# First layer of a two-model kernel: POOL's elementwise parts moved to DVE, squares ahead of weight splits, decays regrouped

## What is computed

```python
hn = rms_norm(h, norm_mix_g[0])
xx = token_shift(x) - x                       # x is hn
xr, xw, xk, xv, xa, xg = [x + xx * mix[i] for i in range(6)]
r, k, v = xr @ w_r, xk @ w_k, xv @ w_v
w_log = -softplus(-(w0 + tanh(xw @ w1) @ w2)) - 0.5
a = sigmoid(a0 + (xa @ a1) @ a2)
g = sigmoid(xg @ g1) @ g2
kk = heads(k * k_k); kk = kk / maximum(norm(kk), 1e-12)
k = k * (1 + (a - 1) * k_a)
decay = exp(-exp(w_log))                      # then the scan with r, decay, k, v, -kk, kk * a
```

## Time and profile before

| | |
|---|---|
| median of 3 runs | 3311.23 us (3302.97 to 3314.74) |
| the profiled execution | 3308.2 us, its span 3306.0 us |
| PE busy | 3093.4 us (94%) |
| DVE busy | 1885.4 us (57%) |
| ACT busy | 1278.8 us (39%) |
| POOL busy | 698.1 us (21%) |
| mean granted clock of PE | 0.964 |
| chain that ended last | PE 75%, DVE 13%, ACT 4%, DMA 3%, issue 2%, POOL 1% |

### The profile page before, as it was taken

How to read it: one execution, slowest core, us unless ns; L and a number is a source line. 1 busy time by engine, 2 the same in 40 slices (tenths; PEclk the granted TensorE clock), 3 DMA queues, 4 the chain that set the end, 5 groups by cost and what they waited for, 6 DMA issues and landing times.

```text
span 3306.0 us, 46816 instructions
## 1 busy us (share of the span) xinstructions
PE 3093.4 (94%) x19356; PEld 2711.4 (82%) x19356; DVE 1885.4 (57%) x2692; ACT 1278.8 (39%) x2186; POOL 698.1 (21%) x682
## 2 busy tenths in 40 slices
PE   5989999999999988889999989898999999999998
PEld 5987878789999978789999987655788887878887
DVE  6676545546666562653666665786553544355353
ACT  3555555433223342553432335432332333243231
POOL 3233222122112240111320231311120211112020
PEclk9889999999999989889999999999999999999999
DMA  2210000024554421002446452100222232222222
GB/s 89 77 53 34 1 1 1 34 84 141 175 182 138 166 68 61 1 1 71 148 149 211 136 183 89 51 1 7 83 88 97 90 102 83 96 83 88 97 90 89
DMA packets 79652, 284.40 MB, mean 86 GB/s; under 512 B 8496, under 2 KB 9392, under 8 KB 78672
## 3 DMA queue, kind: packets, MB, share of 16 engines
q1 hardware_dynamic: 79440, 281.41, 25.4%
HBM read 275.02 MB, written 6.36 MB: 85 GB/s over the span
## 4 chain that ended last, share of the span: by engine, by line
PE 75%; DVE 13%; ACT 4%; DMA 3%; issue 2%; POOL 1%; SPq 0%; DVEq 0%; ACTq 0%; POOLq 0%
PE psum L347 54%; DMA araw<-d_ada 3%; DVE wlo L304 2%; PE psum L1216 2%; PE psum L382 2%; PE psum L1237 1%; DVE xt L692 1%; PE psum L1248 1%; DVE araw L428 1%; DVE rdn L2650 1%; PE psum L1245 1%; PE psum L1920 1%; PE psum L2574 1%; DVE mxw L2629 1%; ACT whi L297 1%
## 5 line engine op out<-in xcount | busy, mean ns | idle before, releaser
L304 DVE TENSOR_TENSOR wlo<-wraw,whi 128x1024 fp32r<-128x1024 f32 (+2 forms) x398 | 526.2, 1349 | 652.5 <-ACT whi L297 644.1
L297 ACT CAST whi<-wraw 128x1024 fp32r<-128x1024 f32 (+2 forms) x398 | 395.7, 1022 | 529.4 <-PE psum L347 482.3
L428 DVE CUSTOM_DVE_ANT_0 araw<-araw,cond 128x1024 f32<-128x1024 f32 x112 | 137.4, 1237 | 82.3 <-DMA araw<-d_ada 82.2
L347 PE MATMUL psum<-f1xh,whi 128*128 128x264 f32 x704 | 144.5, 287 | 7.4 <-DVE f1xl L542 3.9
L347 PE MATMUL psum<-f0xh,whi 128*128 128x264 f32 x704 | 143.9, 286 | 7.9 <-DVE wlo L304 4.1
L347 PE MATMUL psum<-f1xh,wlo 128*128 128x264 f32 x704 | 143.9, 286 | 0.0
L347 PE MATMUL psum<-f3xh,whi 128*128 128x512 f32 x352 | 139.8, 397 | 4.2 <-DVE f3xl L538 4.2
L347 PE MATMUL psum<-f2xh,whi 128*128 128x512 f32 x352 | 139.7, 397 | 4.2 <-DVE f2xl L538 4.2
L347 PE MATMUL psum<-f1xl,whi 128*128 128x264 f32 x704 | 143.5, 285 | 0.0
L347 PE MATMUL psum<-f0xh,wlo 128*128 128x264 f32 x704 | 143.4, 285 | 0.0
L347 PE MATMUL psum<-f0xl,whi 128*128 128x264 f32 x704 | 143.0, 285 | 0.0
(11 more groups left out here) (518 smaller groups left out, 8937.7 us busy)
## 6 DMA issues: line engine op xcount, KB each, us to landing
wraw<-d_w SPq DMA_DIRECT2D x357, 512.0 KB, 3.4
araw<-d_ada SPq DMA_DIRECT2D x112, 512.0 KB, 3.3
wraw<-d_w SPq DMA_DIRECT2D x32, 384.0 KB, 3.1
hn<-d_h SPq DMA_DIRECT2D x4, 528.0 KB, 7.3
hres<-d_h SPq DMA_DIRECT2D x1, 2112.0 KB, 8.4
spill<-hres SPq DMA_DIRECT2D x1, 2112.0 KB, 7.4
hres<-spill SPq DMA_DIRECT2D x1, 2112.0 KB, 8.4
cond<-d_cond SPq DMA_DIRECT2D x2, 1024.0 KB, 4.9
```

Source lines behind the costliest of these rows:

```text
L297: e.copy(whi[0:rows, n % NH, 0:kt * cols], wraw[0:rows, n % NR, 0:kt * cols]).then_inc(*w_hi.up(n))
L304: e.tensor_tensor(wlo[0:rows, n % NH, 0:kt * cols], wraw[0:rows, n % NR, 0:kt * cols], whi[0:rows, n % NH, 0:kt * cols].bitcast(F32), ALU. ...
L347: ins = e.matmul(psum[0:bw, b0 + nb * len(sl) + si, 0:ln], l_ if z == 2 else h_, (xp.lo if z == 1 else xp.hi)[:, k, o:o + ln], start=k == ...
L428: e.tensor_tensor_reduce(out=w, in0=w, in1=self.c[:, col, :], scale=1.0, scalar=0.0, op0=ALU.mult, op1=ALU.add, accum_out=ada[:, ly, blk, ...
```

## The change

It does five things, all in the first layer's projections.

- The low parts of the odd blocks (48 blocks in all, 24 of them on POOL before), the even blocks of `xx`, the decays' subtraction, and the operands `b` and `r` all go from POOL to DVE. POOL keeps one memset here.
- The low part of a block comes one block later than its mix (`rest_dve`), and the weight split between the halves of a mix stands ahead of the half's last low part (`mix_split_dve`).
- At the start ACT squares first, then splits chunks 0 and 1, then takes the root, then splits chunk 2. DVE adds first, then splits chunks 0 and 1; chunk 2 comes after the last mix of k.
- On ACT the decays' exponentials stand two at a time behind each pair of `wr` (0 to 5); 6, 7 and `Fc` go into the operand loop, `square(1)` behind the sigmoids. On DVE decays 6 and 7 go behind mix 3.
- One split on each engine goes behind the small matrix g1's outputs.

```diff
         def mix_dve(e, i, ks):
             for k in ks:
...
-                for q in ([k - 1] if k % 2 else []):
-                    e.wait_ge(*m_hi.at(i, q))
-                    e.tensor_tensor(x.lo[:, q, :], xt_of(i, q), x.hi[:, q, :].bitcast(F32),
-                                    ALU.subtract).then_inc(*m_lov.up(i, q))
+                if k > ks[0]:
+                    rest_dve(e, i, k - 1)
+
+        def rest_dve(e, i, k):
+            x = mixed(i)
+            e.wait_ge(*m_hi.at(i, k))
+            e.tensor_tensor(x.lo[:, k, :], xt_of(i, k), x.hi[:, k, :].bitcast(F32), ALU.subtract).then_inc(*m_lo.up(i, k))
+
+        def mix_split_dve(e, i, ks, n):
+            mix_dve(e, i, ks)
+            w_split_dve(e, n)
+            rest_dve(e, i, ks[-1])
...
-        def mix_pool(e, i, ks=range(1, 8, 2)):
...
             rms_square(e, "r0", lambda k: hn[:, k, 1:L + 1], sq0, lambda e, k: e.wait_ge(d_h4[k // 2], 16), range(8))
+            w_split_act(e, 0)
+            w_split_act(e, 1)
             rms_root(e, "r0", L, rt0, 0)
+            w_split_act(e, 2)
...
                 keep(e, "wr", j, 4 * (j % 2), rT, r_out)
-                if j:
-                    decay(2 * j - 2)
-                    decay(2 * j - 1)
+                if j < 3:
+                    decay(2 * j)
+                    decay(2 * j + 1)
             w_split_act(e, chunk("wv", 0, 1))
...
-            e.wait_ge(*p_sc.at(7, 4))
             square(0)
-            square(1)
-            decay(6)
-            decay(7)
-            e.activation(Fc[:, :, :], fa[:, :, :], ACT.Exp, scale=-KAPPA).then_inc(*p_fc.up(0))
             scale(0)
             scale(1)
...
-            mix_dve(e, 4, range(4))
-            w_split_dve(e, n + NH)
-            mix_dve(e, 4, range(4, 8))
-            w_split_dve(e, n + NH + 1)
+            mix_split_dve(e, 4, lo, n + NH)
+            mix_split_dve(e, 4, hi, n + NH + 1)
...
+                e.tensor_tensor(RA[:, 0, k, :], lc, RA[:, 0, k, :], ALU.subtract).then_inc(*p_sc.up(k, 5))
-            for j in range(4):
+            for j in range(3):
                 w_split_dve(e, chunk("wr", j, 0) + NH - 1)
                 decay(2 * j)
...
+            w_split_dve(e, chunk("wr", 3, 0) + NH - 1)
+            mix_split_dve(e, 3, lo, chunk("wr", 3, 1) + NH - 1)
+            mix_split_dve(e, 3, hi, chunk("wv", 0, 1))
+            decay(6)
+            decay(7)
...
+                e.tensor_tensor(a_, nr, a_, ALU.mult).then_inc(*up("b"))
                 e.wait_ge(*p_ls.at(m))
                 e.tensor_tensor(k_, k_, ls, ALU.mult).then_inc(*up("K"))
-                e.wait_ge(*p_b.at(m))
+                e.wait_ge(*p_op.at("b", m))
                 e.scalar_tensor_tensor(out=a_, in0=a_, scalar=v("kk", m), in1=ls, op0=ALU.mult, op1=ALU.mult).then_inc(*up("B"))
+                e.wait_ge(*p_e.at(m))
+                e.tensor_tensor(rT(m), rT(m), LC_[:, m, :], ALU.mult).then_inc(*up("r"))
```

More of the change, by code:

```diff
@@ L633, in program @@
         d_cr = sem("d_cr")
-        h_n = sig("h_n", [x for k in range(8) for x in ([("n", k)] + ([("x", k)] if k % 2 else []))])
-        xx_p = sig("xx_p", [(k,) for k in range(0, 8, 2)])
+        h_n = sig("h_n", [("n", 0)] + [x for k in range(8) for x in ([("n", k + 1)] if k < 7 else []) + [("x", k)]])
         MT = [(i, k) for i in MIX for k in range(8)]
@@ L638, in program @@
         m_hi = sig("m_hi", MT)
-        m_lov = sig("m_lov", [x for x in MT if x[1] % 2 == 0])
-        m_lop = sig("m_lop", [x for x in MT if x[1] % 2])
+        m_lo = sig("m_lo", MT)
         k_out = sig("kept", [(nb,) for nb in range(8)])
@@ L651, in program @@
         p_s = sig("p_s", [(k,) for k in range(8)])
-        p_sc = sig("p_sc", [(k, i) for k in range(8) for i in range(5)])
-        p_L3 = sig("p_L3", [(k,) for k in range(8)])
+        p_sc = sig("p_sc", [(k, i) for k in range(8) for i in range(6)])
         p_l3 = sig("p_l3", [(k,) for k in range(8)])
@@ L663, in program @@
         p_mka = sig("p_mka", [(0,), (1,)])
-        p_op = sig("p_op", [(s, k) for k in range(8) for s in ("kk", "k", "rk", "s", "K", "B")])
-        p_b = sig("p_b", [(k,) for k in range(8)])
-        p_r = sig("p_r", [(k,) for k in range(8)])
+        p_op = sig("p_op", [(s, k) for k in range(8) for s in ("kk", "k", "rk", "s", "b", "K", "B", "r")])
         p_bon = sig("p_bon", [(k,) for k in range(8)])
         p_sb = sig("p_sb", [(ti,) for ti in range(5)])
-        def mix_lo(i, k):
-            return (m_lop if k % 2 else m_lov).at(i, k)
         def xt_of(i, k):
@@ L956, in proj_act @@
             e.preload_act_table_set("natural_log_exp_and_others")
+            e.wait_ge(*p_sc.at(7, 5))
+            square(1)
             for m in range(8):
@@ L976, in proj_act @@
                 e.activation(lc, lc, ACT.Exp, scale=-KAPPA).then_inc(*p_e.up(m))
+                if m in (0, 1):
+                    decay(6 + m)
+                elif m == 2:
+                    e.activation(Fc[:, :, :], fa[:, :, :], ACT.Exp, scale=-KAPPA).then_inc(*p_fc.up(0))
                 if m % 2:
@@ L990, in proj_dve, with normed @@
             rms_add(e, "r0", sq0)
+            w_split_dve(e, 0)
+            w_split_dve(e, 1)
             e.wait_ge(*n_rf.at("rc", "r0", 1))
             e.wait_ge(*zeroed.at("h", 0))
-            for k in range(8):
+            def normed(k):
                 e.scalar_tensor_tensor(out=hn[:, k, 1:L + 1], in0=hn[:, k, 1:L + 1], scalar=v("nmix0", k), in1=rt0,
                                        op0=ALU.mult, op1=ALU.mult).then_inc(*h_n.up("n", k))
-                if k % 2:
-                    e.wait_ge(*h_n.at("n", k))
-                    e.tensor_tensor(xx[:, k, :], hn[:, k, 0:L], hn[:, k, 1:L + 1], ALU.subtract).then_inc(*h_n.up("x", k))
+            normed(0)
+            for k in range(8):
+                if k < 7:
+                    normed(k + 1)
+                e.wait_ge(*h_n.at("n", k))
+                e.tensor_tensor(xx[:, k, :], hn[:, k, 0:L], hn[:, k, 1:L + 1], ALU.subtract).then_inc(*h_n.up("x", k))
+                mix_dve(e, 2, (k,))
                 if k:
-                    mix_dve(e, 2, (k - 1,))
-            mix_dve(e, 2, (7,))
+                    rest_dve(e, 2, k - 1)
+            w_split_dve(e, 2)
+            rest_dve(e, 2, 7)
+            lo, hi = range(4), range(4, 8)
             w_split_dve(e, NH)
-            mix_dve(e, 1, range(4))
-            w_split_dve(e, NH + 1)
-            mix_dve(e, 1, range(4, 8))
-            w_split_dve(e, NH + 2)
+            mix_split_dve(e, 1, lo, NH + 1)
+            mix_split_dve(e, 1, hi, NH + 2)
             w_split_dve(e, NH + 3)
             n = chunk("w1", 0, 0)
-            mix_dve(e, 4, range(4))
-            w_split_dve(e, n + NH)
-            mix_dve(e, 4, range(4, 8))
-            w_split_dve(e, n + NH + 1)
+            mix_split_dve(e, 4, lo, n + NH)
+            mix_split_dve(e, 4, hi, n + NH + 1)
             lora_dve(e, "w1")
@@ L1733, in program @@
         b_hi = more(m_hi, [(i, k) for i in range(2) for k in range(8)])
-        b_lo = more(m_lop, [(i, k) for i in range(2) for k in range(8)])
+        b_lo = sig("b_lo", [(i, k) for i in range(2) for k in range(8)])
         b_q = sig("b_q", [(hh, d) for hh in range(16) for d in range(2)])
@@ L2837, in _ @@
         def _(e):
-            for n in range(NH):
-                w_split_dve(e, n)
             proj_dve(e)
@@ L2913, in _ @@
         def _(e):
-            for n in range(NH):
-                w_split_act(e, n)
             proj_act(e)
```

77 lines of the change are left out of this document (20 added, 57 removed).

## The result

Eight executions of the kernel before gave a median of 3311.22 us (3302.40 to 3316.02); seven of the changed one a median of 3294.7 us (3283.21 to 3301.74). The ratio is **0.9948, interval 0.9928 to 0.9968**: some 17 us faster. An eighth execution of the changed kernel took 10459.74 us; it is left out of the ratio.

> The changed kernel as it is, for a trace at an ordinary clock. Rival B (only the start wins): the first 10 us are there, and of the rest at most 3 us; PE's wait for the last read-out of wr stays near 6 us or the clock is low during the keys.

The account below looks back on a forecast made before the run. PE, busy 94% of the span, was taken as the bound, with gains only where it waits or its clock is low. 10.6 + 3.8 + 7.0 = 21.4 us off gave 3289.8, stated as 3289; range 3276 to 3299.

Parts of the forecast that it names:

- Rival B: Only the start wins: ACT stays late before `wv`, or PE's clock drops during the keys; 11 us gain, 3300, chance 0.15.
- w2: Small matrix behind the keys: its third block is freed 0.95 us sooner, saving some 0.7 us at the low clock.
- Start: First norm: squares wait only for `hn`, so PE's sums begin near 12.7 us instead of 23.28; gain 10.6 us.
- Mixes: Keys' mix gains 1.0 us, mixes 1, 4, 5, 0 gain 2.1; last keys' read-out 3.1 us earlier, counted from the norm.
- new waits for `wlo`: Sign against the forecast: PE having new waits for `wlo` between 45 and 90 us.
- One sign: Sign for the forecast: no DVE instruction of 528 columns lasts above 0.8 us before 260 us.
- Mix 3 to a's sigmoids: Before `wv`: 3.4 us from PE's `wr` wait, 1.4 from a sigmoid wait, 2.2 from the clock; 7.0 us gain.
- Rival A: PE's clock stays up, so neither `wr` nor `wv` begins at 1.2 GHz; gain 32 us, 3279, chance 0.15.
- Operands: Operand loop: DVE's step falls to 6.5 us from 7.6, but PE is busy throughout; gain 0, at most 0.3 us.
- Rival C: DVE becomes the bound, its long instructions not shrinking when POOL is silent; 17 us slower, 3328, chance 0.04.
- Rival D: The change fails to do what it says: `hn` or a weight chunk late, shift within 10 us; chance 0.03.

Follow-up runs that it names:

- e8: e5's kernel with ACT's rounding of each half's weight chunk moved ahead of that half's last high part; 3278.68 us, ratio 0.9898 to the kernel before.
- e5: Changed kernel with four scalings of a, not two, ahead of ACT's split of a `wv` chunk; 3285.54 us, ratio 0.9927 to the kernel before.
- e6: Changed kernel with decay 6 back ahead of mix 3 on DVE; 3298.22 us, ratio 0.9954 to the kernel before.
- e3: Changed kernel with the operand loop's two products (b and r) back on POOL; 3297.8 us, ratio 0.996 to the kernel before.
- e2: Changed kernel with the old start, weight splits 0 to 2 ahead of squares and additions; 3298.78 us, ratio 0.9973 to the kernel before.

## Why the prediction was right

The median of the first measurement lies 5.7 us above the forecast and inside the range; the direction and the mechanism are those said, with one exception in the operand loop that cost little. Point by point, in us, with the durations before and after in brackets:

| step | forecast | measured |
|---|---|---|
| start, to the first scaling of `hn` | 10.6 | 10.7 (29.98 to 19.27) |
| from there to the last keys | 3.1 | 3.3 (87.26 to 83.97) |
| w2 | 0.7 | 0.2 (13.98 to 13.76) |
| `wr` to its last read-out | 3.4 | 3.4 (58.50 to 55.07) |
| from there to the operand loop | 3.6 | 3.7 (28.59 to 24.88) |
| operand loop | 0, at most 0.3 | 0.8 (59.77 to 59.01) |
| sum | 21.4 | 22.1 |

Two terms were mis-sized, w2 by 0.5 us too much and the operand loop by 0.8 too little. They nearly cancel, which is luck.

*Start.* The sums began 0.4 us later than said (`hn` lands later) but took 4.59 us instead of 5.15. That is luck of the execution: the same twelve matmuls took 4.4 us in e8 and 5.6 in e5. The two errors hid each other.

*Mixes.* The keys' mix took 23.0 us from the first `hn` to the last low part (19.27 to 42.25), for the 23.1 from the root that I had counted. The half of 7.57 us was right to 0.01, and for the reason given: DVE's wait of 1.04 us stays as long as ACT's rounding hangs behind the last mix. The step was costed rightly and read wrongly: I wrote that what POOL gave back "fills DVE's 1.04 us of waiting and the added low part", while the wait of 1.03 us is still there; what POOL gave back went into the added low part alone. e8 is what that row was offering. None of the new waits for `wlo` that would have spoken against me came: PE waits for nothing between 45 and 90 us. One sign was worded too widely: no mix, low part or product on DVE lasts above 0.8 us, but the eight scans of the decays, of 528 columns too, take 1.25 us, as they did before.

*w2.* The 0.7 us for the block freed earlier measured 0.2. ACT frees it earlier, but then has the moved split of weights in the way: its sigmoids begin 6.64 us behind the read-out of the last keys in both traces (123.88 after 117.24, 109.88 after 103.24). Then the last three come 1.32 us apart, as before, at PE's pace: ACT waits 0.62 us for PE before each, with the clock at half.

*Mix 3 to a's sigmoids.* PE's wait, forecast at 3.2 us, measured 3.4, one wait for `BT` of 1.8 is left, and the clock gave back 2.3 us where I had taken 2.2. That 2.2 was a choice between ends of 4.8 and 12.9 for the whole term, so its hitting is partly luck; e6, with a wait 2.1 us longer, lost 7.1. *Rival A* failed on the clock: half from 173.6 to 180.4 us, full, half again from 187.2 to 190.6. e5 and e8 show how much of A was there to be had: without the wait the second drop is missing.

*Operands.* The bound of 0.3 us was too small by 0.5, and e3 gives it back: the loop is 59.8 us with POOL's products and 59.0 without. The step that failed is the one from PE's 62.09 of 63.00 busy us to a gain of 0: DVE was nearly as full as PE there, never waited, and was the one that paced the loop. In the change the first steps are paced by DVE (6.6 us apart), the later ones by PE (7.2 to 7.4, the last 8.9).

*Rival C* needed DVE's long instructions to stay long. In this trace all of the 48 mixes last 0.75 to 0.77 us. The Trainium skill, Perfetto Trace Analysis, "Optimizing Scalar/DVE Operations", warns that work moved between DVE and GpSimd might not help because they share a port; by that, the trace agrees, with e3's 1.15 us of standing for each product.

*Rival B* falls with e2, and the granted clock stays at 1.00 from 30.2 to 108.7 us, through all of the keys. *Rival D* falls with the start: the last of `hn` landed in time for a square at 11.88 us, and PE waited for no chunk of weights longer than before (1.5 and 0.6 us, for 1.7 twice). The chances, by the cases as written, make 0.88 for faster and not 0.89.

**What stays open.** By the trace the change is worth 22.1 us in one execution after another (layer's end at 255.96, 256.10, 255.91 us), by medians 16.5, 18.9 and 23.1 us. The forecast of a single profiled execution was met to 0.5 us (3286.8; 3286.33 taken), but that is luck too: the two others traced took 3279.73 and 3279.33. Behind the first layer the same instructions took 3028.5, 3021.8 and 3021.6 us in three executions of one kernel, and 3027.9 in both of before. The mean granted clock of the executions varies with the time (in the first set 0.967 at 3283.21 us, 0.966 at 3287.62, 0.958 at 3298.39). So the scatter goes with the clock, and where traces can be compared it lies behind 260 us. Whether the change touches the clock there is not shown, and the longest executions (3305 to 3312 us) were none of those traced.

## What to carry to other kernels

Where two engines stand in each other's way, look for small instructions that last as long as the other engine's large one: a product of one column that took 1.32 us said that POOL's product already cost DVE more than making it would (1.2 us for 0.7). When the engine has a wait that returns before the same step in every half, ask what the releaser did last and whether that needs the late input: e8 gained some 7 us from the order on ACT, the low parts' move to DVE about 4. When PE is busy 99% of a stretch, look whether another one is too: in the operand loop it was DVE that had no wait. And read the gain of a short edit from a mark inside the trace (here the layer's end, the same to 0.2 us), since here the ratio of one kernel came out at 0.9925 to 0.9954 in three sets, with the differences lying behind that mark.

## What the runs showed of the hardware

- A wait of 1.8 us of PE was followed by a low clock of 3.4 us in the change and of 13.7 us in e6, and removing it removed the second drop (e5, and its repeat). Short matmuls on 64 partitions with pauses of 0.7 to 1.7 us go with a clock of half around w2, in before and in the change, with PE busy 9.80 of 12.30 us in the change; in e8, with one pause of 1.2 us there, the drop is 6.8 us long and not 13.7.
- A clock of 1.00 in these views can mean that nothing was recorded. The trace of before has no record of the clock until 27.8 us, and that of the change none until 16.5, where the record goes to 1.00; the sums' matmuls in front of these marks start 0.44 us apart and behind them 0.22, so the clock was at half before. This switch came at different times in different executions, and the sums took 4.4 to 5.6 us by it.
- In the execution of 10459.74 us the first sums took 10.20 us instead of about 5, and the 128x264 matmuls of L347 had a mean of 587 ns instead of 285. In its `wr` matmuls start 0.42 us apart, where other traces show 0.12 at a clock of 1.00 and 0.22 at 0.50, so PE was slower than at either level. Its trace holds no record of the clock at all, and the view's 1.00 says nothing. DVE was busy 1851.5 us, about as long as otherwise (1865.8). The page and the timeline:

```profile
span 10457.9 us, 46793 instructions
PE 10368.2 (99%) x19356; PEld 7865.2 (75%) x19356; DVE 1851.5 (18%) x2744; ACT 1310.8 (13%) x2185; POOL 602.1 (6%) x630
13.37 10.20 PE L505 MATMUL psum<-r0sq,cst 128*128 128x264 f32 x12 [13.37 <-DVE r0sq L475]
```

It happened in one of 26 executions of this kernel, and nothing in the runs says why.
